# Moving the scaling of the modulation weights out of the two mixing stages and into three feed-forward parts

## What is computed

```python
silu_c = jax.nn.silu(c); silu_cc = jax.nn.silu(c_ctx)
h, hc = x, ctx                                  # x: what the first block gave
for i in range(DEPTH):                          # DEPTH = 2
    sh1, sc1, g1, sh2, sc2, g2 = split(silu_c @ mod_w[i] + mod_b[i], 6)
    a = rmsnorm(h, norm1_w[i]) * (1 + sc1) + sh1
    if i == 0:                                  # the context is read in layer 0 only
        csh1, csc1, ... = split(silu_cc @ mod_w[i] + mod_b[i], 6)
        ac = rmsnorm(hc, norm1_w[i]) * (1 + csc1) + csh1
    m = ab_mixer(a, ac, ...) if i == 0 else hyena_mixer(a, ...)
    h = h + g1 * m
    u = rmsnorm(h, norm2_w[i]) * (1 + sc2) + sh2
    h = h + g2 * ((silu(u @ w1[i]) * (u @ w3[i])) @ w2[i])
return rmsnorm(h, final_norm_w)
```

## Time and profile before

| | |
|---|---|
| median of 3 runs (lowest, highest) | 2469.78 us (2468.61, 2473.2) |
| profiled execution | 2467.38 us, its span 2465.6 us |
| busy in the span | PE 93%, DVE 51%, ACT 27%, POOL 2% |
| chain of work that ended last | PE 75%, DVE 17%, ACT 5%, issue 2%, DMA 1% |
| mixing of layer 0, the eight units that carry steps | about 373 to 462 us |
| ffn0, ffn1, ffn2, ffn3 | from about 492, 1166, 1798 and 2252 us |

### The profile page before, as it was taken

The page is one execution under the profiler, slowest core; times in us unless marked ns, Lnnn a source line. Parts: engine busy times, 40 slices in busy tenths (PEclk is TensorE's granted clock), DMA queues, the critical chain, the costliest instruction groups (busy, mean ns, idle before and its releaser), DMA issues.

```text
span 2465.6 us, 33483 instructions
## 1 busy us (share of the span) xinstructions
PE 2293.0 (93%) x14158; PEld 1902.1 (77%) x14158; DVE 1259.1 (51%) x2224; ACT 659.3 (27%) x882; POOL 57.5 (2%) x79
## 2 busy tenths in 40 slices
PE   6999989999989999799999998898899989989997
PEld 5858768699978587686999687877489967546996
DVE  3341346688733413444888366546355553634544
ACT  1113320043301133200444153321143411003442
POOL 0000000001000000000000000000010000000000
PEclk9999989999999999899999998999899999999999
DMA  6433326678644332267785321110265542203551
GB/s 212 150 111 115 116 81 226 209 252 279 211 135 149 120 119 103 86 222 249 244 281 201 92 73 65 36 36 2 63 188 187 171 141 79 97 0 115 186 186 68
DMA packets 207754, 348.68 MB, mean 141 GB/s; under 512 B 20643, under 2 KB 111562, under 8 KB 207221
## 3 DMA queue, kind: packets, MB, share of 16 engines
q1 hardware_dynamic: 192704, 291.15, 34.9%
q0 software_dynamic: 14624, 55.31, 6.8%
q10 hardware_dynamic: 276, 0.08, 0.0%
HBM read 345.48 MB, written 1.05 MB: 141 GB/s over the span
## 4 chain that ended last, share of the span: by engine, by line
PE 75%; DVE 17%; ACT 5%; issue 2%; DMA 1%; SPq 0%; DVEq 0%; ACTq 0%
PE psum L375 53%; PE psum L716 20%; DVE ring_low L1042 4%; DVE A L1506 3%; DVE G L1169 2%; ACT high_weights L1035 1%; DVE wide_room L1169 1%; ACT A L819 1%; PE psum L434 1%; DVE A L1169 1%; DVE tmp L1169 1%; DMA ring<-in_w_in_dram 1%; PE psum L420 1%; PE psum L694 0%; DVE xn L1469 0%
## 5 line engine op out<-in xcount | busy, mean ns | idle before, releaser
L375 PE MATMUL psum<-hT,ring 128*128 128x256 f32 (+1 forms) x3472 | 689.4, 360 | 16.3 <-DVE G L1169 7.1
L375 PEld LDWEIGHTS psum<-hT,ring 128*128 128x128 f32 x3472 | 602.5, 196 | 92.7 <-DVE G L1169 7.3
L1042 DVE TENSOR_TENSOR ring_low<-ring,high_weights 128x2048 fp32r<-128x2048 f32 x124 | 284.2, 2292 | 169.6 <-ACT high_weights L1035 167.6
L716 PE MATMUL psum<-high_rows,high_weights 128*128 128x256 f32 x1280 | 364.1, 284 | 4.8 <-DVE ring_low L1042 4.8
L716 PE MATMUL psum<-high_rows,ring_low 128*128 128x256 f32 x1280 | 362.4, 283 | 0.0
L716 PEld LDWEIGHTS psum<-high_rows,high_weights 128*128 128x128 f32 x1280 | 242.5, 189 | 7.0 <-issue 6.3
L716 PEld LDWEIGHTS psum<-high_rows,ring_low 128*128 128x128 f32 x1280 | 244.7, 191 | 0.0
L1035 ACT ACTIVATE high_weights<-ring 128x2048 fp32r<-128x2048 f32 x124 | 237.8, 1917 | 3.9
L1506 DVE SCALAR_TENSOR_TENSOR A<-A,silu_c 128x256 f32<-128x256 f32 x392 | 190.1, 485 | 14.0
L716 PE MATMUL psum<-yT_low,high_weights 128*128 128x256 f32 x640 | 181.2, 283 | 0.0
L716 PE MATMUL psum<-x2T_low,high_weights 128*128 128x256 f32 x640 | 180.1, 281 | 0.0
(11 more groups left out here) (409 smaller groups left out, 2485.5 us busy)
## 6 DMA issues: line engine op xcount, KB each, us to landing
ring<-in_w_in_dram SPq DMA_DIRECT2D x36, 2048.0 KB, 7.7
ring<-in_ffn_w_dram SPq DMA_DIRECT2D x66, 1024.0 KB, 5.3
A<-in_mod_w_dram POOLq DMA_DIRECT2D x48, 1024.0 KB, 7.7
ring<-in_ffn_w_up_dram SPq DMA_DIRECT2D x44, 1024.0 KB, 5.3
ring<-in_ffn_w_down_dram SPq DMA_DIRECT2D x22, 1024.0 KB, 6.9
ring<-in_w_lift_dram SPq DMA_DIRECT2D x16, 1024.0 KB, 8.4
ring<-in_ab_w_in_dram SPq DMA_DIRECT2D x7, 2048.0 KB, 7.9
ring<-in_hy_w_in_dram SPq DMA_DIRECT2D x6, 2048.0 KB, 8.0
```

Source lines behind the costliest of these rows:

```text
L375: return pe.eng.matmul(out, lhsT, rhs, start=(k == 0), stop=(k == n - 1))
L716: ins = pe.eng.matmul(out, lhs[a], rhs[b], start=first and n == 0, stop=last and n == 2)
L1042: v.eng.tensor_tensor(low, whole, high.bitcast(F32), ALU.subtract).then_inc(*v.mark(f"w_lo/{l}.{i}"))
```

## The change

Every step is kept, with the same operations; what changes is when it is done. The eight units of each mixing stage carry no step any more. ffn0 does steps 0 to 11 (one for each column step, two at `j` = 9), ffn1 steps 12 to 27 (two for `j` = 0 to 4, one for 5 to 10), ffn2 steps 28 to 47 (two for `j` = 0 to 8, one for 9 and 10). Steps 0 to 7 have two rows still. The steps of ffn2 use rooms of their own (ztok and x1tok, and a corner of wide_room for the sums), since A1 to A3 are gone by then. POOL loads the steps of a part in order: the first two of ffn0 and ffn1 behind `hgrn_ready`, the first two of ffn2 behind the sums of squares of ffn2, which use ztok, and behind the Hyena constants. The gains of layer 1 are made at the end of ffn2, inside `ffn_dve` behind the last `modulation_done`; that of layer 0's second norm is made at the start of the second block.

```diff
@@ modulation_steps
-    if l >= DEPTH or j >= FFN_STEPS:
+    if l not in MODULATIONS or j >= FFN_STEPS:
         return []
-    two = 16 - FFN_STEPS
-    return [24 * l + 8 + i for i in ([2 * j, 2 * j + 1] if j < two else [two + j])]
+    first, twice = MODULATIONS[l]
+    at = lambda j_: first + j_ + sum(1 for z in twice if z < j_)
+    return list(range(at(j), at(j + 1)))
+
+MODULATIONS = {0: (0, (9,)), 1: (12, (0, 1, 2, 3, 4)), 2: (28, tuple(range(9)))}
+
+def first_modulation(l):
+    return MODULATIONS[l][0] if l in MODULATIONS else 2 * 24
@@ first_block
-    top["mod_room"] = [z[:, :].rearrange("p (k c) -> p k c", k=KD) for z in (A1, A3)]
-    mod_acc = A2[:, 0:1024].rearrange("p (i w c) -> p i w c", i=2, w=2)
+    top["mod_room"] = {0: [z[:, :].rearrange("p (k c) -> p k c", k=KD) for z in (A1, A3)]}
+    top["mod_sum"] = {0: A2[:, 0:1024].rearrange("p (i w c) -> p i w c", i=2, w=2)}
+    mod_acc = lambda i: top["mod_sum"][int(i >= first_modulation(2))][:, i % 2, :, :]
+    mod_room = lambda i: top["mod_room"][int(i >= first_modulation(2))][i % 2]
@@ tensor, mixing
                 for q in range(4):
                     merge_unit(l, n, q)
-                    if (n, q) != (2, 0):
-                        modulation_summed(pe, banks, 24 * l + 4 * (n - 2) + q - 1)
...
-            modulation_summed(pe, banks, 24 * l + 7)
             ffn_tensor(l, f"ffn{l}")
@@ dve, mixing
                     merge(l, n, q)
-                    i = 24 * l + 4 * (n - 2) + q
-                    if (n, q) != (2, 0):
-                        modulation_done(v, i - 1)
-                    modulation_scaled(v, i)
...
-            modulation_done(v, 24 * l + 7)
@@ ffn_dve
             if l == 1 and j == 0:
-                top["gains"](range(3))
+                top["gains"](range(2))
...
         for i in modulation_steps(l, FFN_STEPS - 1):
             modulation_done(v, i)
+        if l == 2:
+            top["gains"](range(3, 5))
@@ second_block
+    top["mod_room"][1] = [z[:, :, :].rearrange("p t d -> p (t d)").rearrange("p (k c) -> p k c", k=KD) for z in (x1tok, ztok)]
+    top["mod_sum"][1] = wide_room[:, 11 * 1024:].rearrange("p (i w c) -> p i w c", i=2, w=2)
@@ second block, dve
-        gains(range(3, 5))
+        gains([2])
@@ gpsimd
+            def modulation_in(i):
+                if i >= 2:
+                    pool.wait_ge(*reached(f"mod_acc/{i - 2}"))
+                src = io["mod_w_2"][i // 24][:, (i % 24) * 256:(i % 24 + 1) * 256].rearrange("(k p) c -> p k c", p=P)
+                pool.eng.dma_start(top["mod_room_of"](i), src).then_inc(*pool.loads(f"mod_in_{i % 2}/{i}"))
...
             for l in range(DEPTH):
                 pool.wait_ge(*reached(f"hgrn_ready/{l}.1"))
-                for i in range(24 * l, 24 * l + 24):
-                    if i == 24 + 9:
+                for i in range(first_modulation(l), first_modulation(l + 1)):
+                    modulation_in(i)
+                    if i == first_modulation(1) + 1:
                         pool.wait_ge(*reached("merged/1.3.3"))
                         pool.eng.dma_start(second["ctx_in"], ...)
...
             for n in range(ORDERS):
+                if n:
+                    pool.wait_ge(*reached("sumsq/ffn2.1"))
+                    for i in range(first_modulation(2), first_modulation(3)):
+                        modulation_in(i)
                 for half in range(2):
```

More of the change, by code:

```diff
@@ L342, in first_block @@
     A1, A2, A3 = sb("A1", [P, 2048]), sb("A2", [P, 2048]), sb("A3", [P, 2048])
-    top["mod_room"] = [z[:, :].rearrange("p (k c) -> p k c", k=KD) for z in (A1, A3)]
-    mod_acc = A2[:, 0:1024].rearrange("p (i w c) -> p i w c", i=2, w=2)
+    top["mod_room"] = {0: [z[:, :].rearrange("p (k c) -> p k c", k=KD) for z in (A1, A3)]}
+    top["mod_sum"] = {0: A2[:, 0:1024].rearrange("p (i w c) -> p i w c", i=2, w=2)}
+    mod_acc = lambda i: top["mod_sum"][int(i >= first_modulation(2))][:, i % 2, :, :]
+    mod_room = lambda i: top["mod_room"][int(i >= first_modulation(2))][i % 2]
+    top["mod_room_of"] = mod_room
     score = sb("score", [P, SEQ])
@@ L693, in modulation_summed @@
             for c in range(2):
-                ins = pe.eng.matmul(b[:, 2 * c + which:2 * c + which + 1], mod_acc[:, i % 2, which, c * P:(c + 1) * P],
+                ins = pe.eng.matmul(b[:, 2 * c + which:2 * c + which + 1], mod_acc(i)[:, which, c * P:(c + 1) * P],
                                     consts["ones"][:, 0:1], start=True, stop=True)
@@ L1496, in modulation_scaled @@
         v.wait_ge(*reached("silu_c/1"))
-        w = top["mod_room"][i % 2]
+        w = mod_room(i)
         for which in range(mod_rows(i)):
-            acc = mod_acc[:, i % 2, which, :]
+            acc = mod_acc(i)[:, which, :]
             for k in range(KD):
@@ L3087, in _ @@
             pool = Worker(eng, "pool", marks)
+            def modulation_in(i):
[3 more added lines that the diff above has]
+                pool.eng.dma_start(top["mod_room_of"](i), src).then_inc(*pool.loads(f"mod_in_{i % 2}/{i}"))
+                marks.at[f"mod_in/{i}"] = marks.at[f"mod_in_{i % 2}/{i}"]
             for l in range(DEPTH):
                 pool.wait_ge(*reached(f"hgrn_ready/{l}.1"))
-                for i in range(24 * l, 24 * l + 24):
-                    if i == 24 + 9:
+                for i in range(first_modulation(l), first_modulation(l + 1)):
+                    modulation_in(i)
+                    if i == first_modulation(1) + 1:
                         pool.wait_ge(*reached("merged/1.3.3"))
                         pool.eng.dma_start(second["ctx_in"], io["ctx_2"][0].rearrange("(t p) d -> p t d", p=P)).then_inc(*pool.loads("ctx_in/0"))
[L3095 to L3099, removed]
             pool.wait_ge(*reached("x/1.3"))
```

## The result

| | before | after |
|---|---|---|
| median of the runs (lowest, highest) | 2471.49 us (2468.61, 2473.87), 4 runs | 2508.54 us (2507.91, 2509.15), 4 runs |
| profiled execution | 2467.38 us | 2508.06 us |
| span | 2465.6 us | 2506.3 us |

The ratio is 1.0148, 95% interval 1.0134 to 1.0162: the change makes the kernel 37 us (33 to 40) slower. 2504 was predicted, +34.6 on the profiled execution; the median before, then of three runs, stood 1.7 us lower.

A forecast was written before the change was run, and what follows sets the result against it. PE holds the chain for three quarters of the span, but DVE and ACT bound rounds with two modulations. Terms -7.9 + 5.1 - 0.4 + 37.8 = +34.6 us on 2467.4 give 2502.0, forecast as a 2504 median, range 2494 to 2513.

The forecast's parts named there:

- A column step costs the longer of PE's time and DVE's round: ffn parts: PE's 16.95 us, plus 0.33 for each summed row, against DVE's round, 18.90 with two rows, 14.67 with one.
- the work hides in ffn2: ffn2, rival: DVE's waits for ACT can be filled, PE stays the bound; +3.6 us in all, 2473; chance 4%.
- The mixing pays only for PE's sums: Mixing stages: seven of eight sums in each layer saved, -7.9 us; removing DVE's covered scaling and the loads gives nothing.
- the loads had held up panels: Mixing, rival: the loads that leave were slowing panels, so the mixing gains 5 us more; 2499 us; chance 5%.
- ffn0: A(0) to A(10) of ffn0 becomes 178.2 us where it was 173.1: +5.1.
- ffn1: ffn1: same pattern of steps, one gain vector less in each of two places, 0.2 us each: -0.4.
- The filter layers: ffn2, j = 4, 6, 8: DVE's operations 3.20 us and wait for ACT 3.24 make rounds of 25.34 us each.
- they stay covered: ffn2 filter rounds, rival: PE or ACT run ahead and take up 6.4 us in each of three; 2485 us; chance 7%.
- The loads: ffn2: 20 MB more cost zero; rival: they come late in the first round, 3 to 7 us, 2507 to 2511; chance 9%.
- The last round: ffn2, j = 9: one row, two bias additions, no further pieces: 10.24 us.
- The end of ffn2: End of ffn2: the residual waits for a sum behind PE's down products, starting 16.96 us behind A(10), not 10.15: +6.8.
- The clock falls for whole rounds: ffn2 behind the filter layers, rival: PE's work takes 35 us at 1.2 GHz, +10 for each of three; 2534; chance 3%.

The follow-up runs named there:

- e1: Changed kernel with the 20 steps of ffn2 scaling only the first of their eight blocks; loads and sums stay: 2483.87 us, ratio 1.0041 to the kernel before.
- e2: Changed kernel with one step a column step in ffn2, the last 9 steps left out with loads and sums: 2480.44 us, ratio 1.0031 to the kernel before.
- e5: Kernel before without the 16 steps of the mixing stages, left out with loads, sums and bias additions: 2464.79 us, ratio 0.9975.
- e3: Changed kernel with DVE's filter layer in front of the scaling of the same column step, all work done: 2499.37 us, ratio 1.0108 to the kernel before.
- e7: Changed kernel with the filter layers in column steps 3, 5, 7 in place of 4, 6, 8: 2508.41 us, ratio 1.0153 to the kernel before.
- e4: Changed kernel with the last column step's sums between the token halves in ffn0, ffn1 and ffn2: 2498.32 us, ratio 1.0104 to the kernel before.
- b4: Kernel before with the last column step's sums between the two token halves in ffn0 and ffn1: 2467.76 us, ratio 0.9984.
- p1: Kernel before with ffn0 and ffn1 laid as two steps in column steps 0 to 5, one in 6 to 9, none in the last: 2474.02 us, ratio 1.0012.

## Why the prediction was right

Its main terms held, by the stretches and by the experiments.

- *A column step costs the longer of PE's time and DVE's round.* Right: rounds of 18.51, 18.72, 18.90 and 14.67 us were forecast to 0.02 us from rows of ffn0 (one round of 19.00 excepted), and e1 and e2 show the threshold from the other side. The rival that the work hides in ffn2 is out, by 33 us; so is "each step costs its share", by e2.
- *The mixing pays only for PE's sums.* Right, mis-sized: 9.4 us (6.2 + 3.1), not 7.9. The piece of the chain that a sum makes is shorter than what it adds to the distance of two units, 0.79 against 0.89 us. The distance is the row to take. The rival that the loads had held up panels is out, by PE's rows under e5.
- *ffn0* +5.5 for +5.1, *ffn1* -0.2 for -0.2.
- *The filter layers* came to 25.66, 25.28 and 25.65 us for 25.34. One of DVE's eight operations took 0.66 us in place of 0.28 in two of the three rounds (more on it at the end); the wait for ACT is 3.21 for 3.24. e3 shows that it is a matter of order alone. The rival that they stay covered is out.
- *The loads* landed in time; no row of DVE in ffn2 waits for one. That rival is out. In e1 all 20 loads of ffn2 stay, and PE sets the pace.
- *The last round* is the step that failed, by 1.7 us: 11.94 for 10.24. The prediction said that a clock at half for 3 to 4 us leaves the gate and up products "ready about 7 us early". That holds where a full round follows. The round of j = 9 prepares no further pieces and is 8 us shorter, so there is no slack; and the half clock lasted 5 us. e7 takes this wait away, e3 most of it (0.35 us is left).
- *The end of ffn2* had the right mechanism: +7.3 for +6.8. The later residual is only 5.2 of it, so that the sum came near has luck in it: 2.1 us more lie behind the residual, for which the prediction had nothing and whose cause is open. e4 takes back 5.8.
- *The clock falls for whole rounds*: out. It was back at 1.00 after 4 to 5 us of PE's work each time. But the prediction's picture of it was wrong in two points. It had PE idle for 7 us in a filter round; it idled 3.2, 2.8 and 3.2 us, and 1.0 to 2.4 us in the rounds between. And it held the mean clock of 0.98 in ffn0 against a clock that falls at every column step. PE does not wait in every round there, but twice in those five, and behind the first wait it ran at half clock (behind the second, of 0.93 us, it did not). PE's first matmul behind that wait, and a row by stages:

```profile
561.32 0.36 PE L716 MATMUL psum<-high_rows,high_weights 128*128 128x256 f32 x1 [1.04 <-DVE ring_low L1042]
```

```profile
563.00:565.00 2.00, 2.00 (x11) 2.00 (x11) 1.19 (x2) 0.40 (x1) 0.00 (x0) 0.50 1.05 406
```

In ffn2 of the changed kernel all of the last six column steps begin at 1.2 GHz, behind waits of 1.0 to 3.2 us. The shorter kind, in the same two views:

```profile
1937.84 0.36 PE L725 MATMUL psum<-high_rows,high_weights 128*128 128x256 f32 x1 [1.10 <-issue]
```

```profile
1939.00:1941.00 2.00, 2.00 (x11) 2.00 (x11) 1.10 (x2) 1.40 (x1) 0.00 (x0) 0.50 1.01 369
```

The loop whose passes all start cold, which the prediction cites from the Trainium skill, "TensorE: Matmul & The Clock Gate", section "HAM oscillation — how this bites in real kernels", agrees with these six column steps, and ffn0 does not speak against it as the prediction had it. In five of the six the half clock cost nothing, since DVE's round was the longer one.

Predicted +34.6, measured 37 (33 to 40). The terms of the touched stretches sum to 36.6 us; the rest of the 40.7 by which the two profiled executions differ is the untouched stretches. The medians differ by 37.

I believed one thing that the forecast did not need: that ffn1's end, like ffn0's, holds up what follows. It is what made e4, b4 and p1 smaller than expected.

## What to carry to other kernels

Room on an engine is not its idle share. It is what is left between the bound engine's time for a round and the other's whole serial round, with its waits for a third engine in it: here 6.5 us of a round in which DVE was idle for 8, and the step that did not fit cost its full excess in every round. Spread such filler so that each round stays below the threshold, put what a third engine must answer ahead of the filler and not behind it, and leave the last round free; and look at what comes behind a wait (the context's projection behind ffn1) before counting its end as a gain.

## What the runs showed of the hardware

- PE's half clock (1.2 GHz), where it lay on the path, cost 1.7 us in the last gate and up products of the changed kernel and 1.6 us in the last down products of e7. The length of PE's idle does not settle whether it comes. The changed kernel has it behind idles of 1.02 and 1.10 us and not behind the 2.82 us at the end of ffn2. At the end of ffn1 the same 36 matmuls stand behind the same idle of 2.85 us, first in the kernel before (granted clock 1.00), then in the changed one (0.50 between 1362 and 1364):

```profile
1363.25 8.56 PE psum L716 x36
```

```profile
1361.75 9.93 PE psum L725 x36
```

What decides it no run here shows.

- PE's clock can fall in a stretch in which PE is busy without a gap. The first 208 fp32 matmuls of the second block took 49.28 us in the kernel before (mean granted clock 0.90) and 50.92 in b4 (0.87). In the kernel before, 32 matmuls of 16 columns start at 1408.44, PE is busy throughout, and it is granted 0.50 from about 1413 to 1423. Seven of the twelve kernels have the 49.28, five the 50.92. It is 1.6 us of the up to 4.8 by which nearly identical code between ffn1 and ffn2 differs (459.8 to 464.6 us).
- One TENSOR_SCALAR of 64 x 256 (the filter's, line 1537 of the changed kernel) took 0.66 us in two of its three rounds there and in e4, 0.66 to 0.67 in all three in e2 and in e7, and 0.64 in one of three in e1; in the other kernels it took 0.28 to 0.29 each time. DVE's row in the round of j = 4 and in that of j = 6, and the rows of POOL, which issues the next step's load (start, us, line, operation), in the changed kernel:

```profile
1907.30 0.66 DVE L1537 TENSOR_SCALAR tmp<-tmp 64x256 f32<-64x256 f32 x1
```

```profile
1951.86 0.28 DVE L1537 TENSOR_SCALAR tmp<-tmp 64x256 f32<-64x256 f32 x1
```

```profile
1906.99 0.88 POOL L3101 DMA_DIRECT2D ztok<-in_mod_w_dram  x1 [3.15 <-DVE wide_room L1512]
...
1952.12 0.88 POOL L3101 DMA_DIRECT2D ztok<-in_mod_w_dram  x1 [3.36 <-DVE wide_room L1512]
```

In the long case the instruction starts 0.31 us into POOL's issue and lies within it but for its end; in the short one it is over when the issue begins or just after. All eleven long cases start 0.30 to 0.34 us into an issue. In e3 the filter runs ahead of the scaling, and no issue of a load stands beside it. That POOL's issue holds DVE up is a guess from these times; no run tests it. A TENSOR_SCALAR of 0.29 us that starts at 1952.18, 0.06 us into an issue, was not held up, nor were two in e1 that start 0.7 us into one. It stays open, and weighs 0.4 us a round.
